# Gate and up of the feed-forward part as seven half-size products per 128 columns, in three of four groups

## The chip, the cores and the metric

One core of one Trainium2 chip. The time is the device time of one launch in microseconds; of the kernel before three runs are known, 3519.23, 3510.82 and 3515.81 us, median 3515.81 us. The profile is of a further execution of 3516.95 us, whose span from the first to the last instruction is 3515.2 us.

## The reference, cut to what matters

One decoder layer runs over 16 meta tokens, 8 short sequences of 4 tokens and a prompt of 2048 tokens: input projection, sliding-window attention and a gated delta rule side by side, their merge, an output projection, and the feed-forward part, which the change is about:

```python
D_MODEL = 1024
D_FF = 2816
hn = _rms_norm(h, norm_ffn)
h = h + (jax.nn.silu(hn @ w_gate) * (hn @ w_up)) @ w_down
```

All of it is float32.

## The kernel before, in words

**Groups.** The prompt is worked through in four groups (`NG`) of 512 tokens. The first group carries the 48 other tokens too (16 meta, 32 of the short sequences), so it is 560 tokens wide, and each of its products is made in two halves of 280 columns (`CA`, `CB`). Activations lie with features on the partitions and tokens along the columns (`MAIN` is the 512 prompt tokens of a group).

**Precision.** TensorE multiplies in a rounded 32-bit format (fp32r). To keep float32 accuracy each operand is split into a rounded part and the rest: ACT makes the rounded part of a weight tile (`weights_hi`, L521, `wh`), DVE the rest (`weights_lo`, L529, `wl`), and each 128x128 weight tile takes three products: rounded x rounded, rounded x rest, rest x rounded (`t_out`, all of them recorded at L768).

**The weight stream.** All weights come in units of 128 partitions x 1024 columns (512 KB, eight 128x128 tiles), 120 per group in the order of `UNITS`, the same for each group: input projection, conv, gates, z, oa/ob, eight `out` units, then for each half `cc` of the feed-forward width (`FFC` = 2 halves of `FFK` = 11 column blocks): `wg` and `wu` of each block, then 11 `down` units. SP loads them (L511) into a ring of two (`raw`), each load waiting until the rest of the unit two before has been made (`lo_done`). Split units lie in a ring of three (`wh`, `wl`); ACT splits unit n+2 once TensorE has begun unit n (`unit_started`, `AHEAD` = 2), and DVE follows it.

**Order on an engine.** Each engine runs its instructions in the order in which they are written; waits on semaphores (`made(...)`) tie them together. Calls `hi_until` (ACT) and `lo_until` (DVE) put the splits of coming units ahead of the step that follows them.

**The feed-forward part.** In the `out` phase DVE adds each of eight output tiles to the residual (`add_columns`, L2114); ACT scales it by the norm's weight and rounds it (L1584, `hnT[0]`), DVE makes the rest (`hn_lo`, L2101, `hnT[1]`), and squares are summed for the norm (L2110). TensorE starts `wg` of block 0 at once, and after it sums the squares over the partitions (L447); DVE (L2141) and POOL (L1679) turn that into one factor per token, which TensorE spreads over the partitions after `wu` of block 0 (L453), and DVE copies it to `hR` (L2145). For each block j: 24 products for gate and 24 for up, each 512 columns wide (in the first group 48 and 48 of 280); DVE multiplies gate by `hR` (L2153, `sg`), ACT applies silu (L1595), DVE multiplies up by `hR` (L2161, `hf`) and then by `sg` (L2165), ACT rounds it (L1598) and DVE makes the rest (L2167) for `down`. Two banks of PSUM each alternate for gate and up, so DVE has a whole block to read them. During the second `down` phase the next group's tokens are loaded and normed.

## Time and profile before

| | |
|---|---|
| median of three runs | 3515.81 us |
| profiled execution / its span | 3516.95 us / 3515.2 us |
| TensorE busy with products | 3422.6 us, 97% of the span, 21860 products |
| DVE, ACT, POOL busy | 1729.8 us (49%), 1256.7 us (36%), 253.2 us (7%) |
| DMA | 298.66 MB, mean 85 GB/s |
| one group's feed-forward part (second group) | from 1505.8 us to about 1874 us |

Products overlap in TensorE, so the duration of one in the profile is longer than the time until the next one starts; where it runs without a pause, the stretch divided by the number of products gives the distance between them. The columns of the windows view are: stretch, length, then for each engine the busy time and in brackets the number of instructions, the granted clock of TensorE as a share of 2.4 GHz, the DMA's busy share and its GB/s.

### The profile page before, as it was taken

To read this page: it belongs to the slowest core of one execution; us is meant where nothing else is said; L and a number is where in the kernel's file an instruction comes from. 1 tells how busy PE (TensorE), PEld (TensorE's weight loads), DVE (VectorE), ACT (ScalarE), POOL (GpSimd) and SP (SyncE) were. 2 spreads that over 40 slices of the span, in tenths; PEclk is the share of its full clock that TensorE was granted. 3 is DMA by queue.
4 is the path that set the end of the run, shared out by engine and by line. 5 is a ranking of instruction groups with operands and counts; after the bars stand their busy time and mean duration, and the time that the engine had idled before them with its cause. 6 is when DMAs were issued, how large, how long until landed. Compare 5 with 4: busy or idle time off the path is not lost.

```text
span 3515.2 us, 52951 instructions
## 1 busy us (share of the span) xinstructions
PE 3422.6 (97%) x21860; PEld 2907.3 (83%) x21860; DVE 1729.8 (49%) x3115; ACT 1256.7 (36%) x2414; POOL 253.2 (7%) x289
## 2 busy tenths in 40 slices
PE   7989999999999999999999999999999999999998
PEld 6877789999998777888878877888878877788886
DVE  4734335543447654544446744554345754454343
ACT  3323334321234544432233544432223544432222
POOL 2211000000003110000002101000000311000000
PEclk9988899999999999999999999999999999999999
DMA  4201013222233111333243211333334211233232
GB/s 172 67 27 56 25 37 99 86 90 85 85 132 112 56 42 50 114 96 96 91 143 110 68 39 47 108 96 96 96 116 139 79 37 43 78 114 96 96 96 81
DMA packets 88574, 298.66 MB, mean 85 GB/s; under 512 B 12288, under 2 KB 14288, under 8 KB 87680
## 3 DMA queue, kind: packets, MB, share of 16 engines
q1 hardware_dynamic: 88336, 295.28, 26.2%
q8 instruction: 175, 2.87, 0.3%
q14 instruction: 63, 0.52, 0.0%
HBM read 283.63 MB, written 12.62 MB: 84 GB/s over the span
## 4 chain that ended last, share of the span: by engine, by line
PE 52%; issue 11%; ACT 2%; DMA 1%; DVE 1%; SPq 0%; POOLq 0%; POOL 0%; DVEq 0%; ACTq 0%
PE bank L768 43%; PE bank L956 1%; PE bank L1193 1%; PE bank L1184 1%; PE bank L1196 1%; PE bank L931 1%; PE bank L1127 1%; PE bank L943 1%; DMA raw<-in_wstream 1%; PE bank L1101 1%; PE bank L1107 0%; PE bank L984 0%; ACT junk L1542 0%; PE bank L1029 0%; PE bank L1138 0%
## 5 line engine op out<-in xcount | busy, mean ns | idle before, releaser
L768 PE MATMUL bank<-hnT,wh 128*128 128x512 f32 (+1 forms) x3520 | 931.4, 352 | 0.0
L529 DVE TENSOR_TENSOR wl<-raw,wh 128x1024 fp32r<-128x1024 f32 x480 | 594.9, 1240 | 653.4 <-ACT wh L521 652.0
L768 PE MATMUL bank<-xnT,wh 128*128 128x512 f32 (+2 forms) x2560 | 742.9, 376 | 10.9 <-DVE d_dT L1955 5.1
L768 PEld LDWEIGHTS bank<-hnT,wh 128*128 128x128 f32 x3520 | 619.4, 188 | 91.4 <-issue 0.2
L521 ACT CAST wh<-raw 128x1024 fp32r<-128x1024 f32 x480 | 500.6, 1043 | 386.5 <-PE bank L768 328.4
L768 PE MATMUL bank<-hnT,wl 128*128 128x512 f32 (+1 forms) x1760 | 622.2, 354 | 0.0
L768 PEld LDWEIGHTS bank<-xnT,wh 128*128 128x128 f32 x2560 | 450.4, 194 | 84.2 <-issue 13.4
L768 PE MATMUL bank<-hid,wh 128*128 128x512 f32 (+1 forms) x1760 | 469.4, 354 | 4.3 <-DVE wl L529 3.1
L768 PE MATMUL bank<-xnT,wl 128*128 128x512 f32 (+2 forms) x1280 | 470.0, 367 | 0.0
L768 PEld LDWEIGHTS bank<-hnT,wl 128*128 128x128 f32 x1760 | 330.6, 188 | 45.8
L768 PEld LDWEIGHTS bank<-hid,wh 128*128 128x128 f32 x1760 | 310.3, 188 | 52.2 <-DVE wl L529 4.7
L768 PE MATMUL bank<-hid,wl 128*128 128x512 f32 (+1 forms) x880 | 311.3, 354 | 0.0
L768 PEld LDWEIGHTS bank<-xnT,wl 128*128 128x128 f32 x1280 | 247.7, 193 | 40.5
L1598 ACT CAST hid<-hf 128x512 fp32r<-128x512 f32 (+1 forms) x88 | 55.5, 630 | 420.2 <-DVE hf L2165 420.2
L768 PEld LDWEIGHTS bank<-hid,wl 128*128 128x128 f32 x880 | 165.9, 189 | 24.1
L768 PE MATMUL bank<-oT,wh 128*128 128x512 f32 (+1 forms) x640 | 169.4, 353 | 4.4 <-DVE oT L2067 3.2
L768 PE MATMUL bank<-mixT,wh 128*128 128x512 f32 (+1 forms) x640 | 169.4, 352 | 1.9 <-DVE mixT L2097 1.9
L1595 ACT ACTIVATE sg<-sg 128x512 f32<-128x512 f32 (+1 forms) x88 | 56.5, 642 | 318.2 <-DVE sg L2153 318.2
L768 PE MATMUL bank<-wh,xnT 128*128 128x512 f32 (+1 forms) x544 | 138.8, 343 | 8.0 <-DMA cm<-in_consts 8.0
L768 PEld LDWEIGHTS bank<-oT,wh 128*128 128x128 f32 x640 | 112.4, 188 | 21.5 <-ACT oT L1558 3.8
L768 PEld LDWEIGHTS bank<-mixT,wh 128*128 128x128 f32 x640 | 112.7, 188 | 18.9 <-ACT mixT L1580 2.1
L1847 DVE SCALAR_TENSOR_TENSOR cy<-pre,pr,cy 128x512 f32<-128x512 f32 x144 | 119.6, 830 | 5.1
(309 smaller groups left out, 3897.5 us busy)
## 6 DMA issues: line engine op xcount, KB each, us to landing
raw<-in_wstream SPq DMA_DIRECT2D x472, 512.0 KB, 3.5
xr<-in_x_prompt SPq DMA_DIRECT2D x16, 512.0 KB, 5.6
hT<-in_xT SPq DMA_DIRECT2D x4, 2048.0 KB, 8.5
out_yp_out<-hT SPq DMA_DIRECT2D x16, 512.0 KB, 2.9
xT<-in_xT SPq DMA_DIRECT2D x3, 2048.0 KB, 12.5
raw<-in_wstream SPq DMA_DIRECT2D x8, 528.0 KB, 3.6
xT<-in_xT SPq DMA_DIRECT2D x2, 1024.0 KB, 9.9
Sb<-in_state_delta SPq DMA_DIRECT2D x1, 2048.0 KB, 9.7
```

The costliest lines, as they stand in the source:

```text
L521: act.copy(wh[n % HL][:, 0:m], raw[:, n % RAW, 0:m]).then_inc(sem("hi_done"), 1)
L529: nc.vector.tensor_tensor(wl[n % HL][:, 0:m], raw[:, n % RAW, 0:m], wh[n % HL][:, 0:m].bitcast(F32), ALU.subtract).then_inc(sem("lo_done"), 1)
L768: ins = nc.tensor.matmul(*a, **k)
L931: last = nc.tensor.matmul(bank[(1, 2)[half]][:, 256 * (y // NKV):256 * (y // NKV + 1)], qTt[ps, x, :], kT[ps, :, :].rearrange("p s n -> p ...
L943: last = nc.tensor.transpose(bank[b][:, P * y:P * (y + 1)], sc[:, x, P * s:P * (s + 1)], c("ident"))
L956: last = nc.tensor.matmul(bank[4][:, HD * y:HD * (y + 1)], pTm[:, 2 * y + s, :], vn[:, s, ps], start=s == 0, stop=s == 1)
L1101: last = nc.tensor.matmul(bank[(5, 7)[y]][dst, w * h:w * (h + 1)], M[src, 2 * h + z, :], Y[src, 2 * h + z, :], start=True, stop=True)
L1127: last = nc.tensor.matmul(bank[(3, 6)[y]][dst, w * h:w * (h + 1)], X[src, 2 * h + z, :], PT[src, 2 * h + z, :], start=True, stop=True)
L1184: last = nc.tensor.matmul(bank[ob][:, P * x:P * (x + 1)], WQ[:, x, P * k:P * (k + 1)], S[:, x, :], start=x == 0, stop=False, skip_group_ch ...
L1595: act.activation(sg[j % 2][:, live], sg[j % 2][:, live], ACT.Silu).then_inc(sem("sg_done"), 1)
L1598: act.copy(hid[0][:, jj, live], hf[j % 2][:, live]).then_inc(sem("hid_hi"), 1)
L1847: ins = v_.scalar_tensor_tensor(out, src(i), w(i), out, ALU.mult, ALU.add)
```

## The change

In groups 2 to 4, blocks 1 to 21 (`PLAIN` = 1 keeps block 0 as it was) no longer make gate and up as two products of full size. Write the block's weights as a 2x2 matrix: row 1 is gate, row 2 is up, and the columns are the two halves of the 1024 features (A11, A12; A21, A22), and the activations as 2x2: feature halves by token halves (256 tokens each). Then seven products of half the features by half the tokens replace eight (a variant of Strassen's algorithm). Each is one `operand_pass`: four 128x128 tiles x three products = 12 products of 256 columns. The four weight sums S1 to S4 and the four sums of activations are new operands.

- The weight sums are made once, in the first group: SP loads the `wg` and `wu` units of each block a second time (`ops_in`), POOL makes the four sums (`ops_out`), and SP writes them to a DRAM tensor `wsum` (1 MB per block). Later groups load S1 to S4 from it and A11, A12, A22 from the weight stream.
- The stream's unit is now 512 columns (`st`) in these blocks; the rings keep their size in bytes: four cells of 512 columns for `raw`, six for `wh` and `wl`. A full unit takes two cells. `AHEAD` is worked out per unit: up to five `st` units ahead.
- The activation sums are made by DVE in the `out` phase (`token_sums`, from `gS`, the scaled residual) and split like the others (`Tm`): ACT four times 1024 columns after the last `hn_lo`, DVE four times.
- PSUM: the passes A11, S2, S3 and A22 add up in one bank (X), S1 and S4 in another (Z), A12 in a third (Y). Values in between are needed as well, so ACT copies the bank (256 columns) after A11, S1, S2 and S3 (`snap`), and TensorE may not add to that bank before. DVE puts the outputs together from these copies and the final banks. Silu, product and split of block j-1 are done between the steps of block j.
- Some semaphores are merged; nothing else of it changes.

```diff
+PLAIN = 1
+OPS = ("A11", "S1", "S2", "S4", "S3", "A12", "A22")
+SUMS = ("S1", "S2", "S3", "S4")
+HC = 512
+def units_of(g):
+    u = ([("a1", i) for i in range(4)] + [("a2", i) for i in range(2)] + [("conv", j) for j in range(NCONV)]
          + [("gate", j) for j in range(16)] + [("z", j) for j in range(4)]
          + [(s, i) for i in range(4) for s in ("oa", "ob")]
          + [("out", i) for i in range(8)])
-for _c in range(FFC):
-    UNITS += [(s, _c * FFK + j) for j in range(FFK) for s in ("wg", "wu")]
-    UNITS += [("down", _c * FFK + i) for i in range(FFK)]
-UNIT_AT = {u: n for n, u in enumerate(UNITS)}
+    for c in range(FFC):
+        for j in range(c * FFK, (c + 1) * FFK):
+            u += [("wg", j), ("wu", j)] if g == 0 or j < PLAIN else [("st", len(OPS) * j + p) for p in range(len(OPS))]
+        u += [("down", c * FFK + i) for i in range(FFK)]
+    return u
...
+RAWC, HLC = 4, 6
...
+def displaced(n, ring):
+    return max(OWNER.get(c - ring, -1) for c in OWNED[n])
+OWNED = [[] for _ in UNITS]
+for _c, _n in OWNER.items():
+    OWNED[_n].append(_c)
+AHEAD = []
+for _n in range(NU):
+    _m = AHEAD[-1] if AHEAD else 0
+    while _m + 1 < NU and displaced(_m + 1, HLC) < _n:
+        _m += 1
+    AHEAD.append(_m)
...
+    def source(n):
+        g, s, i = UNITS[n]
+        if s != "st":
+            return d["wstream"][STREAM[(s, i)]][:, 0:width(n)]
+        j, op = i // len(OPS), OPS[i % len(OPS)]
+        if op in SUMS:
+            return d["wsum"][j][:, HC * SUMS.index(op):HC * (SUMS.index(op) + 1)]
+        u, half = {"A11": ("wg", 0), "A12": ("wg", 1), "A22": ("wu", 1)}[op]
+        return d["wstream"][STREAM[(u, j)]][:, HC * half:HC * (half + 1)]
     def load_until(sp, n):
-        while asked[0] <= min(n, NG * NU - 1):
+        while asked[0] <= min(n, NU - 1):
             k = asked[0]
-            if k >= RAW:
-                sp.wait_ge(sem("lo_done"), k - RAW + 1)
-            m = width(k % NU)
-            sp.dma_start(raw[:, k % RAW, 0:m], d["wstream"][k % NU][:, 0:m]).then_inc(sem(f"raw_in{k % RAW}"), 16)
+            if displaced(k, RAWC) >= 0:
+                sp.wait_ge(sem("lo_done"), displaced(k, RAWC) + 1)
+            sp.dma_start(raw_cell(k), source(k)).then_inc(sem(f"raw_in{CELL[k] % RAWC}"), 16)
...
+        SNAP = {"A11": 1, "S1": 2, "S2": 3, "S3": 4}
+        snap_of = lambda j, op: len(SNAP) * (j - PLAIN) + SNAP[op]
+        RD = {"Z": 1, "Y": 2, "X": 3}
+        rd_of = lambda j, b: len(RD) * (j - PLAIN) + RD[b]
+        BX, BZ, BY = (lambda j: (0, 3)[j % 2]), (lambda j: (1, 4)[j % 2]), (lambda j: (2, 5)[j % 2])
...
+                for j in range(2 * FFK):
+                    weights("wu", min(j + 1, FFK - 1) if j < FFK else j)
+                    if j == 0:
+                        sp.wait_ge(*made("out_ps", 2 * KD))
+                    if j >= 2:
+                        sp.wait_ge(*made("st_sum", j - 1))
+                        sp.wait_ge(*made("st_out", 16 * (j - 2)))
+                        sp.dma_start(d["wsum"][j - 2], ops_out[:, j % 2].rearrange("p s n -> p (s n)")).then_inc(sem("st_out"), 16)
+                    sp.wait_ge(*made("st_in", 32 * j))
+                    for x, name in enumerate(("wg", "wu")):
+                        sp.dma_start(ops_in[:, j % 2, x, :], d["wstream"][STREAM[(name, j)]][:, 0:2 * HC]).then_inc(sem("st_in"), 16)
+                weights("down", FFK)
+                for j in range(2 * FFK - 2, 2 * FFK):
+                    sp.wait_ge(*made("st_sum", j + 1))
+                    sp.wait_ge(*made("st_out", 16 * j))
+                    sp.dma_start(d["wsum"][j], ops_out[:, j % 2].rearrange("p s n -> p (s n)")).then_inc(sem("st_out"), 16)
...
+            def operand_pass(j, op, b, rhs, start=False):
+                w_h, w_l, mm = unit("st", len(OPS) * j + OPS.index(op))
+                out = bank[b][:, 0:HT]
+                for k in range(KD // 2):
+                    ks = slice(P * k, P * (k + 1))
+                    mm(out, w_h[:, ks], rhs(0, k), start=start and k == 0, stop=False, skip_group_check=True)
+                    mm(out, w_h[:, ks], rhs(1, k), start=False, stop=False, skip_group_check=True)
+                    last = mm(out, w_l[:, ks], rhs(0, k), start=False, stop=k == KD // 2 - 1, skip_group_check=True)
+                last.then_inc(sem("st_ps"), 1)
+            def hn_part(k0, cs):
+                return lambda s, k: hnT[s][:, k0 + k, cs]
+            def T_part(j, q):
+                if j == PLAIN:
+                    pe.wait_ge(*made("hn_hi", KD + q + 1))
+                    pe.wait_ge(*made("hn_lo", KD + q + 1))
+                return lambda s, k: Tm[s][:, q, k, :]
+            def seven_products(j):
+                X, Z, Y = BX(j), BZ(j), BY(j)
+                claim(X, "st_rd", rd_of(j, "X"))
+                operand_pass(j, "A11", X, hn_part(0, H1), True)
+                claim(Z, "st_rd", rd_of(j, "Z"))
+                operand_pass(j, "S1", Z, T_part(j, 0), True)
+                pe.wait_ge(*made("snap", snap_of(j, "A11")))
+                operand_pass(j, "S2", X, T_part(j, 1))
+                pe.wait_ge(*made("snap", snap_of(j, "S1")))
+                operand_pass(j, "S4", Z, hn_part(KD // 2, H2))
+                pe.wait_ge(*made("snap", snap_of(j, "S2")))
+                operand_pass(j, "S3", X, T_part(j, 2))
+                claim(Y, "st_rd", rd_of(j, "Y"))
+                operand_pass(j, "A12", Y, hn_part(KD // 2, H1), True)
+                pe.wait_ge(*made("snap", snap_of(j, "S3")))
+                operand_pass(j, "A22", X, T_part(j, 3))
...
+                    act.copy(hnT[0][:, f, live], gS[:, f, :]).then_inc(sem("hn_hi"), 1)
...
+            if not first:
+                act.wait_ge(*made("hn_lo", KD))
+                for q in range(4):
+                    act.copy(Tm[0][:, q], Ts[:, q]).then_inc(sem("hn_hi"), 1)
...
+            def seven_silu(j):
+                act.wait_ge(*made("ga_done", j + 1))
+                act.activation(sg[j % 2][:, live], sg[j % 2][:, live], ACT.Silu).then_inc(sem("sg_done"), 1)
+            def seven_hid(j):
+                act.wait_ge(*made("hf_done", j + 1))
+                act.copy(hid[0][:, j % FFK, live], hf[j % 2][:, live]).then_inc(sem("hid_hi"), 1)
+            def seven_copies(j):
+                behind = j > PLAIN and j % FFK > 0
+                for op in OPS:
+                    hi_until("st", len(OPS) * j + OPS.index(op))
+                    if op not in SNAP:
+                        continue
+                    act.wait_ge(*made("st_ps", product(j, op)))
+                    if op == "A11":
+                        act.wait_ge(*made("hf_done", j - 1))
+                    elif op == "S1" and j > PLAIN:
+                        act.wait_ge(*made("st_rd", rd_of(j - 1, "Y")))
+                    elif op == "S3":
+                        act.wait_ge(*made("hid_lo", j - 1))
+                    dst = {"A11": sg[j % 2][:, H1], "S1": V[:], "S2": sg[j % 2][:, H2], "S3": hf[j % 2][:, H2]}[op]
+                    act.copy(dst, bank[BZ(j) if op == "S1" else BX(j)][:, 0:HT]).then_inc(sem("snap"), 1)
+                    if op == "A11" and behind:
+                        seven_silu(j - 1)
+                    if op == "S2" and behind:
+                        seven_hid(j - 1)
+                if j % FFK == FFK - 1:
+                    seven_silu(j)
+                    seven_hid(j)
...
+            for j in range(2 * FFK if first else 0):
+                pool.wait_ge(*made("st_in", 32 * (j + 1)))
+                if j >= 2:
+                    pool.wait_ge(*made("st_out", 16 * (j - 1)))
+                A = {f"A{1 + x}{1 + y}": ops_in[:, j % 2, x, HC * y:HC * (y + 1)] for x in range(2) for y in range(2)}
+                Q = {n: ops_out[:, j % 2, SUMS.index(n), :] for n in SUMS}
+                tt = nc.gpsimd.tensor_tensor
+                link(tt(Q["S1"], A["A21"], A["A22"], ALU.add))
+                link(tt(Q["S2"], Q["S1"], A["A11"], ALU.subtract))
+                link(tt(Q["S4"], A["A12"], Q["S2"], ALU.subtract))
+                tt(Q["S3"], A["A11"], A["A21"], ALU.subtract).then_inc(sem("st_sum"), 1)
...
+            def scaled_columns(f):
+                dve.wait_ge(*made("out_ps", f + 1))
+                link(v_.tensor_tensor(hT[:, f, MAIN], hT[:, f, MAIN], bank[(0, 3, 1, 4)[f % 4]][:], ALU.add))
+                v_.tensor_scalar(gS[:, f, :], hT[:, f, MAIN], p("nffn", f, 1), None, ALU.mult).then_inc(sem("h_done"), 1)
+            def token_sums(f):
+                T, k, m = (lambda q, k: Ts[:, q, k, :]), f - KD // 2, KD // 2
+                dve.wait_ge(*made("h_done", f + 1))
+                if f == m - 1:
+                    dve.wait_ge(*made("kv_out", 16 * 2))
+                    step(v_.tensor_tensor(Ts[:, 0], gS[:, 0:m, HT:], gS[:, 0:m, 0:HT], ALU.subtract))
+                elif f >= m:
+                    step(v_.tensor_tensor(T(2, k), gS[:, f, HT:], gS[:, k, HT:], ALU.subtract))
+                    settle()
+                    link(v_.tensor_tensor(T(1, k), gS[:, f, HT:], T(0, k), ALU.subtract))
+                    step(v_.tensor_tensor(T(3, k), gS[:, f, 0:HT], T(1, k), ALU.subtract))
...
+            if not first:
+                for q in range(4):
+                    dve.wait_ge(*made("hn_hi", KD + q + 1))
+                    v_.tensor_tensor(Tm[1][:, q], Ts[:, q], Tm[0][:, q].bitcast(F32), ALU.subtract).then_inc(sem("hn_lo"), 1)
...
+            def seven_up(j):
+                dve.wait_ge(*made("st_ps", product(j, "A22")))
+                v_.tensor_tensor(hf[j % 2][:, H1], bank[BX(j)][:, 0:HT], hR[:, H1], ALU.mult).then_inc(sem("st_rd"), 1)
+            def seven_product(j):
+                dve.wait_ge(*made("sg_done", j + 1))
+                dve.wait_ge(*made("st_rd", rd_of(j, "X")))
+                settle()
+                v_.tensor_tensor(hf[j % 2][:, live], hf[j % 2][:, live], sg[j % 2][:, live], ALU.mult).then_inc(sem("hf_done"), 1)
+            def seven_rest(j):
+                dve.wait_ge(*made("hid_hi", j + 1))
+                v_.tensor_tensor(hid[1][:, j % FFK, live], hf[j % 2][:, live], hid[0][:, j % FFK, live].bitcast(F32), ALU.subtract).then_inc(sem("hid_lo"), 1)
+            def seven_sums(j):
+                behind = j > PLAIN and j % FFK > 0
+                R, gj, uj = hR, sg[j % 2], hf[j % 2]
+                for op in OPS:
+                    lo_until("st", len(OPS) * j + OPS.index(op))
+                    if op == "A11" and behind:
+                        seven_up(j - 1)
+                    elif op == "S2" and behind:
+                        seven_product(j - 1)
+                    elif op == "S3":
+                        dve.wait_ge(*made("st_ps", product(j, "S4")))
+                        dve.wait_ge(*made("snap", snap_of(j, "S2")))
+                        v_.tensor_tensor(gj[:, H2], gj[:, H2], bank[BZ(j)][:, 0:HT], ALU.add).then_inc(sem("st_rd"), 1)
+                        if behind:
+                            seven_rest(j - 1)
+                    elif op == "A12":
+                        dve.wait_ge(*made("snap", snap_of(j, "S3")))
+                        link(v_.tensor_tensor(uj[:, H2], uj[:, H2], V[:], ALU.add))
+                        step(v_.tensor_tensor(uj[:, H2], uj[:, H2], R[:, H2], ALU.mult))
+                    elif op == "A22":
+                        dve.wait_ge(*made("st_ps", product(j, "A12")))
+                        v_.tensor_tensor(gj[:, H1], gj[:, H1], bank[BY(j)][:, 0:HT], ALU.add).then_inc(sem("st_rd"), 1)
+                        dve.wait_ge(*made("st_rd", rd_of(j, "Y")))
+                        v_.tensor_tensor(gj[:, live], gj[:, live], R[:, live], ALU.mult).then_inc(sem("ga_done"), 1)
+                if j % FFK == FFK - 1:
+                    seven_up(j)
+                    seven_product(j)
+                    seven_rest(j)
```

## Rows read from the trace of the kernel before

**Rows 1.** The page: busy time of each engine over the span.

```profile
PE 3422.6 (97%) x21860; PEld 2907.3 (83%) x21860; DVE 1729.8 (49%) x3115; ACT 1256.7 (36%) x2414; POOL 253.2 (7%) x289
```

**Rows 2.** Chain of waits, 1500 to 1640 us: start, length, what.

```profile
1518.86 121.17 PE bank L768 x524
```

**Rows 3.** Windows over gate-and-up stretches, products that read hnT alone; first group, then second.

```profile
666.30:790.10 123.80, 123.79 (x960) 1.00 0.29 89
1518.60:1629.60 111.00, 110.99 (x480) 1.00 0.32 96
1691.00:1813.00 122.00, 122.00 (x528) 1.00 0.28 87
```

**Rows 4.** Windows, all engines: PE, PEld, DVE, ACT, POOL, clock, DMA share, GB/s.

```profile
666.30:790.10 123.80, 123.80 (x963) 123.80 (x962) 58.04 (x85) 33.84 (x42) 0.00 (x0) 1.00 0.29 89
1518.60:1629.60 111.00, 111.00 (x483) 90.23 (x482) 54.55 (x63) 32.99 (x42) 0.00 (x0) 1.00 0.32 96
```

**Rows 5.** Groups by form of the narrow products, whose mean is not their distance.

```profile
L768 PE MATMUL bank<-wh,xnT 128*128 128x264 f32 x272 | 50.5, 284 | 0.0
L768 PE MATMUL bank<-xnT,wh 128*128 128x48 f32 x256 | 44.5, 272 | 5.1 <-DVE d_dT L1955 5.1
```

**Rows 6.** Windows, PE alone: 96 products of 264 columns; 24 of 48 columns.

```profile
1900.80:1912.50 11.70, 11.70 (x97) 1.00 0.53 175
482.20:484.80 2.60, 2.60 (x25) 1.00 0.05 9
```

**Rows 7.** Groups by form: ACT and DVE with 256 columns out of PSUM.

```profile
L1360 ACT COPY qkv<-bank 128x256 f32<-128x256 f32 x16 | 6.0, 374 | 13.4 <-PE bank L768 13.4
L1759 DVE TENSOR_TENSOR qkv<-bank,st 128x256 f32<-128x256 f32 x32 | 13.6, 423 | 90.6 <-PE bank L956 90.6
```

**Rows 8.** Timeline, second group, block 0: start, duration, engine, line, idle before.

```profile
1520.40 0.63 ACT L1595 ACTIVATE sg<-sg 128x512 f32<-128x512 f32 x1 [10.19 <-DVE sg L2153]
1520.94 1.04 ACT L521 CAST wh<-raw 128x1024 fp32r<-128x1024 f32 x1
1522.01 1.23 DVE L529 TENSOR_TENSOR wl<-raw,wh 128x1024 fp32r<-128x1024 f32 x1 [1.64 <-ACT wh L521]
1523.15 0.68 DVE L2161 TENSOR_TENSOR hf<-bank,hR 128x512 f32<-128x512 f32 x1
1523.97 0.69 DVE L2165 TENSOR_TENSOR hf<-hf,sg 128x512 f32<-128x512 f32 x1
```

**Rows 9.** Timeline, second group, from the last out tile to block 1.

```profile
1506.01 0.69 DVE L2114 TENSOR_TENSOR hT<-hT,bank 128x512 f32<-128x512 f32 x1 [1.39 <-PE bank L768]
1512.34 0.16 DVE L2141 TENSOR_SCALAR hr<-bank 128x4 f32<-128x4 f32 x1 [1.98 <-PE bank L447]
1512.64 1.01 POOL L1679 TENSOR_TENSOR hr<-hr,nhalf 128x4 f32<-128x4 f32 x1 [121.50 <-DVE hr L2141]
1517.80 1.06 PE L453 MATMUL bank<-cm,hr 128*128 128x128 f32 x8
1518.90 0.69 DVE L2145 COPY hR<-bank 128x512 f32<-128x512 f32 x1 [6.39 <-PE bank L453]
```

**Rows 10.** Timeline: a pause of TensorE in the third group.

```profile
2001.42 0.66 PE L984 MATMUL bank<-cm,post 128*128 128x128 f32 x4 [2.17 <-ACT post L1458]
```

**Rows 11.** Windows, PE alone: behind that pause, behind one of 2.11 us, behind a like one.

```profile
2002.70:2006.00 3.30, 3.30 (x29) 0.50 0.02 5
2637.60:2640.90 3.30, 3.30 (x9) 0.50 0.93 384
1191.10:1194.50 3.40, 3.35 (x46) 1.00 0.00 0
```

**Rows 12.** Timeline, second group: POOL and DVE both at work in SBUF.

```profile
1115.22 1.21 POOL L1637 TENSOR_TENSOR rt<-qkv,rope_t 128x320 f32<-128x320 f32 x1
1115.61 1.90 DVE L529 TENSOR_TENSOR wl<-raw,wh 128x1024 fp32r<-128x1024 f32 x1
```

**Rows 13.** DMA issues: count, KB each, median us to landing.

```profile
raw<-in_wstream SPq DMA_DIRECT2D x472, 512.0 KB, 3.5
```

More of the change, by code:

```diff
@@ L305, in program @@
     cst = place("cst", [P, NCONV, NB * (CW - 1)])
-    raw = place("raw", [P, RAW, UW])
-    wh = [place(f"wh{s}", [P, UW], F32R) for s in range(HL)]
-    wl = [place(f"wl{s}", [P, UW], F32R) for s in range(HL)]
+    raw = place("raw", [P, RAWC // 2, UW])
+    wh = [place(f"wh{s}", [P, UW], F32R) for s in range(HLC // 2)]
+    wl = [place(f"wl{s}", [P, UW], F32R) for s in range(HLC // 2)]
     r_xn = region(2 * KD * W * 4)
@@ L312, in program @@
     mixT = [place(f"mixT{s}", [P, KD, W], F32R, r_xn + s * KD * W * 4) for s in range(2)]
+    HT = GROWS // 2
+    Tm = [place(f"Tm{s}", [P, 4, KD // 2, HT], F32R, r_xn + s * 4 * KD // 2 * HT * 4) for s in range(2)]
+    V = place("V", [P, HT], F32, r_xn + 2 * 4 * KD // 2 * HT * 4)
+    assert (2 * 4 * KD // 2 + 1) * HT <= 2 * KD * W
+    ops_in = place("ops_in", [P, 2, 2, 2 * HC], F32, r_xn)
+    ops_out = place("ops_out", [P, 2, len(SUMS), HC], F32, r_xn + 2 * 2 * 2 * HC * 4)
+    assert (2 * 2 * 2 + 2 * len(SUMS)) * HC <= 2 * KD * W
     r_gt = region(16 * W * 4)
@@ L516, in weights_hi @@
         assert n == rounded[0]
[L517 to L521 removed]
+        act.wait_ge(sem(f"raw_in{CELL[n] % RAWC}"), 16 * ARRIVED[n])
+        if displaced(n, HLC) >= 0:
+            act.wait_ge(sem("unit_started"), displaced(n, HLC) + 2)
+        act.copy(hi_cell(n), raw_cell(n)).then_inc(sem("hi_done"), 1)
         rounded[0] += 1
@@ L684, in group @@
         last_group = g == NG - 1
+        H1, H2 = slice(NS, NS + HT), slice(NS + HT, W)
+        seven = lambda j: not first and j >= PLAIN
+        product = lambda j, op: len(OPS) * (j - PLAIN) + OPS.index(op) + 1
+        SNAP = {"A11": 1, "S1": 2, "S2": 3, "S3": 4}
[3 more added lines that the diff above has]
+        BX, BZ, BY = (lambda j: (0, 3)[j % 2]), (lambda j: (1, 4)[j % 2]), (lambda j: (2, 5)[j % 2])
         quarters_of = lambda t: QUARTERS_S if t == "S" else QUARTERS_0 if first else QUARTERS
@@ L1381, in gate_logits @@
                 if first:
-                    act.copy(gate[:, j, SM], bank[4][:, B4S:B4S + NS]).then_inc(sem("gate_eS"), 1)
+                    act.copy(gate[:, j, SM], bank[4][:, B4S:B4S + NS]).then_inc(sem("gate_e"), 1)
                 act.copy(gate[:, j, MAIN], bank[0][:]).then_inc(sem("gate_e"), 1)
@@ L1583, in scalar @@
                 act.wait_ge(*made("h_done", (1 + F) * (f + 1)))
-                act.activation(hnT[0][:, f, live], hT[:, f, live], ACT.Copy, scale=p("nffn", f, 1)).then_inc(sem("hn_hi"), 1)
+                if first:
+                    act.activation(hnT[0][:, f, live], hT[:, f, live], ACT.Copy, scale=p("nffn", f, 1)).then_inc(sem("hn_hi"), 1)
+                else:
+                    act.copy(hnT[0][:, f, live], gS[:, f, :]).then_inc(sem("hn_hi"), 1)
                 if f >= 3:
@@ L1592, in scalar @@
                     j = cc * FFK + jj
+                    if seven(j):
+                        seven_copies(j)
+                        continue
                     hi_until("wg", j)
@@ L1609, in scalar @@
                     act.activation((acc if f == 0 else sq[f % 2])[:, live], hT[:, f, live], ACT.Square).then_inc(sem("ysq_done"), 1)
+                    if f == 4 and first:
+                        act.wait_ge(*made("st_out", 16 * 2 * FFK))
                     if f >= 4 and not last_group:
@@ L1701, in lo_until @@
             def lo_until(name, i):
-                while split[0] <= min(g * NU + UNIT_AT[(name, i)] + AHEAD, NG * NU - 1):
+                while split[0] <= AHEAD[NUM[(g, name, i)]]:
                     weights_lo(dve, split[0])
@@ L2135, in vector @@
                     j = cc * FFK + jj
+                    if seven(j):
+                        seven_sums(j)
+                        continue
                     lo_until("wg", j)
```

176 lines of the change are left out of this document (106 added, 70 removed).

## The prediction

> **What bounds the kernel now.** I read the page's busy times first. TensorE is at its products for 97% of the span, DVE for 49%, ACT 36%, POOL 7% [rows 1]. A busy share alone doesn't make a bound, so next the chain of waits in the second group's feed-forward part: from 1518.86 us it is one piece of 121 us of products on TensorE, with no other engine in it [rows 2]. Then the windows over the gate-and-up stretches: busy in all of 111.0 us, granted clock 1.00 [rows 4]. So what counts there is how many products there are and how far apart they start. Divide length by count: 110.99/480 = 231.2 ns and 122.00/528 = 231.1 ns for 512 columns, 123.79/960 = 128.9 ns for the first group's 280 [rows 3]. The other engines have room: in 10 blocks DVE is busy 54.6 of 111 us, ACT 33.0 [rows 4].
>
> **The main term.** A block had 48 products of 512 columns and gets 7 x 12 = 84 of 256. 21 blocks in each of three groups change: 3024 products go, 5292 come. The old ones cost 3024 x 231.1 ns = 698.8 us. No row has 256 columns back to back. The line through 280 and 512 has a slope of (231.1 - 128.9)/232 = 0.4405 ns a column, which gives 128.9 - 24 x 0.4405 = 118.3 ns. The 264-column products start 11.70/96 = 121.9 ns apart [rows 5, 6] and give 121.9 - 8 x 0.4405 = 118.4 ns, the value I take. Bounds: 108 ns, what even 48 columns cost (2.60/24) [rows 5, 6], so a floor under narrow products, and 121.9 ns above. New cost 5292 x 118.4 = 626.6 us, gain **72.2 us** (53.7 at 121.9 ns, 127 at 108). The column work alone falls by an eighth; the gain is less than that, 10%, since each product pays a fixed part (118.4 for 256 against 231.1/2 = 115.6).
>
> The Trainium skill, "TensorE: Matmul & The Clock Gate", section "Back-to-back issue gap", gives N/2.4 + 2.5 ns, so 109.2 ns for 256 columns, and its "LDWEIGHTS" section P/1.2, so 106.7 ns, as the floor. By it the new products would cost 577.9 us, near rival 4. The trace is slower than that formula at both widths it has: 231 against 215.8 ns, and 128.9 against 119.2.
>
> **Does TensorE keep its pace inside a block?** A pass takes 12 x 118.4 ns = 1.42 us, a block 9.95 us. Three times per block a bank may only be added to when ACT has copied it, one pass (1.42 us) after it was filled, and once for bank Z. Durations: an ACT instruction of 512 columns takes 0.63 us but the next starts 0.54 us after it, DVE's 1024 columns 1.23 us with 1.14 between starts [rows 8]: successors overlap by 0.09 us. 256 columns take ACT 0.37 and DVE 0.42 us [rows 7], 0.28 and 0.33 us apart. A DVE instruction that needs the one before it starts 0.14 us after its end (1523.15 + 0.68 to 1523.97) [rows 8]. Per block DVE makes seven splits of 512 columns (0.60 each), three other full-width operations (0.60) and five half-width ones (0.33), with two such pauses: 4.2 + 1.8 + 1.65 + 0.3 = 8.0 us, 80% of a block. ACT: 9 x 0.54 + 4 x 0.28 = 6.0 us. Both fit, but they are in order, so I lay them end to end over a steady block, with A11's start as 0. DVE's last three steps (S3, A12, A22 of the block before) hold 5.1 us of work in 4.3 us, so the gate of block j-1 is complete at 2.0. ACT has copied A11 by then (1.6 to 2.0; needed at 2.84), does silu (to 2.6), the split for step S1 (to 3.2) and the copy of S1 (to 3.5; needed at 4.27). Copy S2: 4.4 to 4.8 (needed 5.69), copy S3: 7.3 to 7.7 (needed 8.54). Each has 0.8 us to spare. The weight splits are up to five passes ahead (7.1 us) and late by 2.9 at most. A load of 512 KB lands after 3.5 us [rows 13]; the new ones are of half that size, and their cells come free 6 us before ACT wants them. Cost: 0, at most the 0.8 us and again as much per block if these spares are gone (rivals).
>
> **The start of each later group's feed-forward part.** Here ACT and DVE get new work that nothing covers. Take the start of `wg` 0 (1505.8 us in the second group) as 0. The new operations in the `out` phase (scaling, three sums of 256 columns per tile) take DVE about 2.1 us per tile; it is idle for 1.39 us ahead of each add [rows 9] and again while ACT splits. Laid end to end behind the last tile, hnT is complete at 4.85, just when TensorE wants it (21 x 0.231). Then ACT rounds the four activation sums (4 x 1024 columns, 0.95 apart: 4.9 to 8.7) and DVE makes their rest (to 10.6), before either turns to weights: ACT splits A11 and S1 (8.7 to 9.8), DVE follows (to 11.7), and only then DVE computes the norm's factor, which it did at 1512.34, that is 6.5 [rows 9]. POOL takes 1.01 us for it [rows 9]: ready at 13.1. TensorE wanted it at 12.0 (1517.80). **1.1 us late.** A11 of block 1 starts at 13.9. Next hR is copied (14.2 to 14.9), gate 0 scaled (15.7), silu 0 (16.3), ACT splits S2 and S4 (17.4), DVE follows (18.1), up 0 and the product (19.6), ACT rounds it (20.3), splits S3 and A12 (21.3) and only then copies A11: 21.6. TensorE would have begun S2 at 16.75, and here a copy can't be late without a cost. **4.9 us.** Behind it ACT is level again. Together 6.0 us x 3 = 18 us. Bounds: 3 if only the first wait stands, 30 if ACT needs a second block to catch up.
>
> Such a pause may drop the clock. After two pauses of some 2.1 us the granted clock was 0.50 (1.2 GHz) for 3.3 us (after one at 2001.42 [rows 10]), after a third it stayed at 1.00 (2.4 GHz) [rows 11]. I count one such stretch per group: half of 3.4 us lost, 1.7 x 3 = 5 us; bounds 0 and 10.
>
> **First group.** POOL makes four sums of 512 columns per block. Its 320 columns took 1.21 us beside DVE [rows 12], so 1.9 us each and 7.7 us per block, in blocks of 96 x 128.9 ns = 12.4 us: it fits, and nothing waits for it but the two last writes. Traffic: two more units read and 1 MB written make 3.1 MB per block, 254 GB/s; 384 GB/s flowed in one window [rows 11]. SP has these DMAs ahead of weight loads, but it is two units (12.4 us) ahead. DVE waits where both want SBUF: 1.90 instead of 1.23 us [rows 12], 0.67 more in four operations per block; with its 58.0 us per 10 blocks [rows 4] that is 8.5 of 12.4 us. Cost: 0. Bounds: 0 and 22.
>
> The Trainium skill, "SBUF — State Buffer", section "SBUF: two separate sides", says that the pair of ports that DVE and GpSimd share is locked for a whole instruction, for DVE also where both inputs are in SBUF; it speaks against moving sums to POOL. The stretched DVE row agrees with it.
>
> **Sum.** 3516.95 (the profiled execution) - 72.2 + 18 + 5 = 3467.8 us. The median of the runs is 1.1 us lower than that execution: **3467 us**, 1.4% less.
>
> **Rivals.**
> 1. *The copies are late by part of a pass in every block.* The estimate above rests on instructions overlapping by 0.09 us. Without that DVE has 9.3 us per block and the spare 0.8 us is used up. Half a microsecond late in 60 blocks: 3467 + 30 = 3497 us. For it: the last three steps already hold more than they can. Against: 2 us of idle DVE in each block. 0.15.
> 2. *The same place, but slower than before.* ACT's copy of S1 comes a whole pass late in each block, since silu, on which it is queued, waits for DVE's gate: 60 x 1.42 = 85 us, so 3552 us. It ends above 3516 once the lateness passes 49/60 = 0.8 us, which needs the gate 1.6 us later than I have it. For and against as in 1; late raw tiles, for which ACT waits in front of a copy, would add to it. 0.11.
> 3. *The shared port slows the first group.* If DVE waits for a whole POOL operation (1.9 us) at each of four operations, a block has 5.8 + 7.6 = 13.4 us of DVE against 12.4: 22 us, 3489 us. Against: the row shows 0.67 us. 0.07.
> 4. *Narrow products come at the 108 ns of the 48-column row.* Gain 127 us, 3412 us. Against it is the line through three widths. 0.03.
> 5. *No difference.* Lateness and start-up eat just the gain. 0.04.
>
> The forecast has 0.60, and its own range is 3450 to 3485 (products at 117.5 to 120 ns, start-up 10 to 27 us). About 0.2% (7 us) is what can be told from no change here. Faster: 0.60 + 0.15 + 0.07 + 0.03 = 0.85, less 0.02 of rival 1's tail: 0.83. Same: 0.05. Slower: 0.12. The range for 8 in 10 runs from 3447 up to 3510, which takes in rivals 1 and 3.
>
> **What would show it.** In the gate-and-up windows of groups 2 to 4: 84 products per block, 9.95 us a block, TensorE without idle time. In a timeline from the last `out` tile: a wait of about 1 us before the spread of the norm's factor and of about 5 us at S2 of block 1, ended by ACT's copy. First group: its stretches still 123.8 and 136 us. It is wrong if passes start over 1.5 us apart in a steady block, and then the releaser tells which: ACT's copy (rivals 1 and 2) or DVE's `wl` (the splits, which I hold to be early).

## The result

3477.79 us is the median of the changed kernel (3474.17 to 3478.18, 4 runs) against 3517.35 us of the kernel before on the same chip (3510.82 to 3519.23, 4 runs): ratio 0.9889, interval 0.9871 to 0.9906, so 1.1% less and clear of no change. The forecast was 3467 us, 1.4% less. The profiled execution has a span of 3475.5 us against 3515.2, so 39.7 us less, at a mean granted clock of 0.979 against 0.981.

The profile after, its page: busy time of the engines, the products of gate and up that read hnT and Tm, and the new loads. It answers to [rows 1] and [rows 13].

```profile
PE 3360.6 (97%) x24128; PEld 2973.7 (86%) x24128; DVE 1974.8 (57%) x3757; ACT 1477.1 (42%) x2993; POOL 388.9 (11%) x377
...
L876 PE MATMUL bank<-Tm,wh 128*128 128x256 f32 x2016 | 372.0, 284 | 13.8 <-DVE wl L609 13.8
...
raw<-wsum SPq DMA_DIRECT2D x252, 256.0 KB, 3.4
raw<-in_wstream SPq DMA_DIRECT2D x189, 256.0 KB, 2.7
```

TensorE stays the bound with 2268 products more (24128 - 21860) and 62 us less busy. DVE went from 49 to 57%, ACT from 36 to 42%. The row of the products that read the activation sums (`Tm`) also holds an idle time: 13.8 us, which is three pauses of 4.6 us.

Windows over the second group's two gate-and-up stretches, all engines for the second and TensorE alone for the first and for two pieces of it (columns as in [rows 4] and [rows 6]):

```profile
1691.44:1801.12 109.68, 109.68 (x924) 109.67 (x923) 86.42 (x158) 70.06 (x139) 0.00 (x0) 1.00 0.59 176
```

```profile
1520.88:1627.72 106.84, 102.26 (x843) 0.97 0.58 173
...
1528.57:1533.50 4.93, 4.93 (x23) 0.50 0.68 205
```

The second stretch is what was forecast for all: 11 blocks of 84 products whose 923 distances fill 109.68 us, so 118.83 ns a product and 9.98 us a block, with no idle time of TensorE. It took 122.00 us before [rows 3]. The first stretch has ten such blocks and should take 839 x 118.83 ns = 99.7 us; it takes 106.84. Its loss sits at block 1, the first one made in seven products. TensorE's timeline there, then ACT's:

```profile
1519.96 1.16 PE L517 MATMUL bank<-cm,hr 128*128 128x128 f32 x8 [0.54 <-POOL hr L1869]
...
1523.71 0.28 PE L876 MATMUL bank<-Tm,wl 128*128 128x256 f32 x1
1528.57 0.80 PE L876 MATMUL bank<-Tm,wh 128*128 128x256 f32 x2 [4.58 <-DVE wl L609]
```

```profile
1523.20 1.12 ACT L602 CAST wh<-raw 128x512 fp32r<-128x512 f32 x2
1526.59 0.62 ACT L1786 CAST hid<-hf 128x512 fp32r<-128x512 f32 x1 [2.27 <-DVE hf L2442]
1527.11 1.13 ACT L602 CAST wh<-raw 128x512 fp32r<-128x512 f32 x2
1528.15 0.36 ACT L1765 COPY sg<-bank 128x256 f32<-128x256 f32 x1
```

The row names DVE's `wl`, which came last by the profile, but the `wl` of this step was there by 1525.13, 3.4 us before; the product that follows starts 0.06 us after the end of ACT's copy of A11 (L1765, 1528.15 + 0.36), which had stood behind block 0's rounding (L1786) and two splits. So it is the queue of ACT that the forecast named. Behind it the clock is 0.50 (1.2 GHz): 23 instructions in 4.93 us, 0.214 us each. The same stretch takes 106.94 and 107.30 us in the third and fourth group: the pause is as long there, 4.58 and 4.60 us, but 5.1 and 6.0 us at half clock lie behind it.

Another pause comes at the end of the same stretch, ahead of the first `down` product. The chain of waits has it in the third group (first fence, columns as in [rows 2]), the timelines of TensorE and then of DVE in the second:

```profile
2327.13 99.52 PE bank L876 x816
2426.65 2.04 issue
2428.70 171.61 PE bank L876 x1189
```

```profile
1627.72 0.28 PE L876 MATMUL bank<-Tm,wl 128*128 128x256 f32 x1
1630.04 0.70 PE L876 MATMUL bank<-hid,wh 128*128 128x512 f32 x2 [2.05 <-issue]
```

```profile
1628.91 0.69 DVE L2400 TENSOR_TENSOR sg<-sg,hR 128x512 f32<-128x512 f32 x1
1629.52 0.42 DVE L2364 TENSOR_TENSOR hf<-bank,hR 128x256 f32<-128x256 f32 x1
1630.30 0.69 DVE L2370 TENSOR_TENSOR hf<-hf,sg 128x512 f32<-128x512 f32 x1 [0.36 <-ACT sg L1744]
```

"issue" says only that the profile shows no releaser. What ends just before is L2364, DVE's last read of bank X of the pass's last block (0.10 us before TensorE starts). That bank is bank 0 in the first pass (block 10, an even number) and bank 3 in the second; `down` claims bank 0 first. The pause is there in the first pass of each later group (2.05, 2.04 and 2.07 us) and in no second pass.

The first group, whose windows answer to [rows 4]:

```profile
666.30:790.10 123.80, 123.80 (x961) 123.59 (x961) 66.69 (x85) 33.94 (x42) 64.19 (x42) 1.00 0.70 247
860.20:996.10 135.90, 135.90 (x1057) 135.90 (x1056) 68.28 (x85) 34.90 (x43) 61.21 (x40) 1.00 0.69 250
```

TensorE has no idle time in it; DVE went from 58.0 to 66.7 us and POOL from nothing to 64.2, both under the products.

**The account.** Gain of the products: 698.8 - 5292 x 0.11883 = 70.0 us. Per later group come off, in distances of starts: 0.8 us ahead of block 1, where the norm's factor is spread (13.85 us from the last `out` product to block 1's first, against 13.04); 7.1 us in the stretch (106.84 - 99.7; 7.2 and 7.6 in the next two groups), of which 4.7 are the pause and 2.4 lie behind it (23 x (0.214 - 0.119) = 2.2 of them are the clock; 2.5 and 2.9 in the next two); 2.2 us ahead of `down` (2.32 instead of a usual 0.11). Over three groups that is 2.4 + 22.0 + 6.6 = 31.0, which leaves 39.0. The two spans counted from the first product of block 1 in the first group differ by 41.5 (2848.9 against 2807.4); of the 2.5 more, 1.2 are the end behind the last `down` product (15.6 us against 16.8), the rest smaller differences up and down. That first product came 1.8 us later in this execution (668.12 against 666.31), and this gives the 39.7. It isn't the change's doing: in two experiments with the same first group it came at 666.28 and 664.67.

### The profile page after: what moved, and what is told of

Its sections match the earlier page's. It is cut to its first block and busy times, and to the rows that moved or that the text cites. A ratio compares the mean times of both kernels' runs of the same rounds, so it can differ in the third digit from the quotient of the medians.

```text
span 3475.5 us, 60004 instructions
## 1 busy us (share of the span) xinstructions
PE 3360.6 (97%) x24128; PEld 2973.7 (86%) x24128; DVE 1974.8 (57%) x3757; ACT 1477.1 (42%) x2993; POOL 388.9 (11%) x377
## 5 line engine op out<-in xcount | busy, mean ns | idle before, releaser
L609 DVE TENSOR_TENSOR wl<-raw,wh 128x512 fp32r<-128x512 f32 (+1 forms) x795 | 750.4, 951 | 644.2 <-ACT wh L602 641.7
L602 ACT CAST wh<-raw 128x512 fp32r<-128x512 f32 (+1 forms) x795 | 636.0, 808 | 483.4 <-PE bank L876 417.5
L876 PE MATMUL bank<-hnT,wh 128*128 128x256 f32 (+2 forms) x3016 | 583.5, 291 | 0.0
L876 PEld LDWEIGHTS bank<-hnT,wh 128*128 128x128 f32 x3016 | 476.3, 189 | 4.3 <-issue 0.2
L876 PE MATMUL bank<-hnT,wl 128*128 128x256 f32 (+2 forms) x1508 | 438.6, 291 | 0.0
L876 PE MATMUL bank<-Tm,wh 128*128 128x256 f32 x2016 | 372.0, 284 | 13.8 <-DVE wl L609 13.8
L876 PEld LDWEIGHTS bank<-Tm,wh 128*128 128x128 f32 x2016 | 313.3, 191 | 14.4 <-ACT sg L1765 14.4
L876 PEld LDWEIGHTS bank<-hnT,wl 128*128 128x128 f32 x1508 | 285.2, 189 | 2.1
L876 PE MATMUL bank<-Tm,wl 128*128 128x256 f32 x1008 | 285.8, 284 | 0.0
L876 PEld LDWEIGHTS bank<-Tm,wl 128*128 128x128 f32 x1008 | 192.2, 191 | 0.0
```

The costliest lines, as they stand in the source:

```text
L602: act.copy(hi_cell(n), raw_cell(n)).then_inc(sem("hi_done"), 1)
L609: nc.vector.tensor_tensor(lo_cell(n), raw_cell(n), hi_cell(n).bitcast(F32), ALU.subtract).then_inc(sem("lo_done"), 1)
L876: ins = nc.tensor.matmul(*a, **k)
```

## The experiments

Time is given as median, ratio to the kernel before on the same chip with its interval, and span. To take out the chance in the beginning, I compare spans counted from the first product of block 1 in the first group ("length"): 2848.9 us before, 2807.4 after. A length is that of one execution. The kernel before took 3514.58 us on the chip of experiments 1, 2, 3 and 5, and 3515.35 us on that of 4, 6, 7 and 8.

**1. The last block's bank X is bank 6, which `down` claims last.**

```diff
-        BX, BZ, BY = (lambda j: (0, 3)[j % 2]), (lambda j: (1, 4)[j % 2]), (lambda j: (2, 5)[j % 2])
+        BX, BZ, BY = (lambda j: 6 if j == FFK - 1 else (0, 3)[j % 2]), (lambda j: (1, 4)[j % 2]), (lambda j: (2, 5)[j % 2])
```

> Bank X of block 10 is bank 6 instead of bank 0. Theory A: the pause of about 2.05 us ahead of the first down unit in each later group comes from its claim on bank 0, which DVE's last read of block 10 (L2364) still holds. Then the three pauses go, and the time falls by 3 x 2.05 = 6 us against the changed kernel (profiled execution about 3470 span). Rival: down waits there for hid (split of the last blocks) or for its weight tiles: then the pauses stay and the time is the same. The cc = 1 start of down, where X is bank 3, has no such pause and doesn't change in either case.

3467.57 us, 0.9866 (0.985 to 0.9883), span 3464.9; length 2798.6, 8.8 less than after. TensorE's timeline at the place of the pause:

```profile
1625.96 0.28 PE L876 MATMUL bank<-Tm,wl 128*128 128x256 f32 x1
1626.07 0.62 PE L876 MATMUL bank<-hid,wh 128*128 128x512 f32 x2
```

The three pauses are gone, so the claim of bank 0 made them: 3 x 2.2 = 6.6 us. The other 2.1 us are a pause ahead of a `down` product at 1814.66 that the changed kernel's trace has and this one hasn't. The kernel before has a like one in the third group [rows 11], and experiment 6, without any seven-product block, has one of 2.07 us there, so it isn't the change's. The pauses at S2 (4.6 us, the third product of block 1) and the clock behind them stay.

**2. Two plain blocks at the start of each later group instead of one.**

```diff
-PLAIN = 1
+PLAIN = 2
...
```

> Block 1 is left plain too (PLAIN = 2). Theory B: the 4.6 us pause at S2 of the first seven-product block is ACT's queue at the start of the part, which is level again a block later. Then it shrinks to about 1 us (block 1's product is rounded 2.4 us after its last product, then two splits, then the copy at 3.8 where 2.84 is wanted), the clock stays at 1.00, and per group 3.6 + 2.5 us come back for 11.1 - 9.98 = 1.1 us given up: 5 us per group, 15 us in all, span about 3460. Rival: every first seven-product block has this pause whatever stands ahead of it, since its first copy always waits for the block before to be finished: then the pause stays at 4.6 us and the time rises by 3.4 us.

3468.10 us, 0.9866 (0.9851 to 0.9881), span 3466.7; length 2798.2, 9.2 less. The pause at S2 and its half clock are gone (22 us in three groups), three blocks fewer have seven products (3 x 1.1 us given back), and new losses take about half of it, so that less came than the 15 us expected: 1.4 to 2.0 us per group in the first stretch, where the first seven-product blocks wait for ACT's copies (0.98 us of it at 1536.55), and the pause ahead of `down`, now 2.6 us, with half a clock behind it in two groups of three. Windows of TensorE over the 3.4 us after that pause, groups 2 to 4:

```profile
1626.52:1629.92 3.40, 3.40 (x9) 0.56 0.33 130
2421.61:2425.01 3.40, 3.40 (x9) 0.53 0.35 122
3217.49:3220.89 3.40, 3.40 (x15) 1.00 0.34 134
```

9 instructions instead of 15 in the first two: 6 x 0.23 = 1.4 us each time.

**3. ACT's and DVE's order around block 0.** The splits for S2 and S4 go ahead of gate and silu of block 0, the copy of A11 of block 1 ahead of the rounding of block 0's product, and that rounding and its rest between the steps of block 1.

```diff
@@ ACT
-                    hi_until("st", len(OPS) * j + OPS.index(op))
+                    if not (j == PLAIN and op == "A11"):
+                        hi_until("st", len(OPS) * j + OPS.index(op))
...
+                    if j == PLAIN and op == "A11":
+                        hi_until("st", len(OPS) * j)
-                    if op == "S2" and behind:
+                    if op == "S2" and j % FFK > 0:
...
+                    if not first:
+                        hi_until("wu", j)
@@ DVE
-                        if behind:
+                        if j % FFK > 0:
...
```

> Only the order on ACT and DVE around block 0 is changed in groups 2 to 4: splits of S2 and S4 ahead of silu 0, the copy of A11 of block 1 ahead of the rounding of block 0's product, that rounding and its rest later, between the steps of block 1. Theory B: the pause at S2 of block 1 falls from 4.6 us to at most 0.5, and with it goes the half clock behind it (2.5 us per group): 3 x 6.6 = 20 us less, span about 3456. The wait of 1 us ahead of the spread stays. Rival: the clock's drop is not a matter of this pause: then only 3 x 4.1 = 12 us go, and the windows behind block 1's start still show 0.5.

3466.80 us, 0.9862 (0.9848 to 0.9877), span 3465.0; length 2797.3, 10.1 less. The window over the first stretch, and TensorE's timeline at its start and ahead of `down`:

```profile
1521.75:1622.11 100.36, 100.30 (x842) 1.00 0.59 180
1622.20:1685.00 62.80, 60.75 (x256) 0.97 0.33 96
```

```profile
1518.70 0.40 PE L876 MATMUL bank<-hnT,wl 128*128 128x512 f32 x1
1520.84 1.16 PE L517 MATMUL bank<-cm,hr 128*128 128x128 f32 x8 [1.74 <-POOL hr L1876]
```

The stretch is 100.4 us instead of 106.8: the 4.58 us and the half clock came from the order of ACT's and DVE's instructions around block 0, 6.5 us here and 5.9 and 6.5 in the next groups, 19 us together, where 20 were expected. Some 8 of them are given back: the norm's factor is later still, since more splits stand ahead of it on DVE (1.74 us of waiting, 15.05 us from the last `out` product), and the 2.05 us ahead of `down` now have half a clock behind them in each group, where they had none in the changed kernel (`down` takes 62.7 us instead of 61.2): 3.6 and 4.6 us in three groups.

**4. The norm's factor right after DVE's first rest of the sums.** The wait and the `tensor_scalar` move from behind the weight splits into the loop over `Tm`, at q = 0.

```diff
+                    if q == 0:
+                        dve.wait_ge(*made("hsum_ps", 1))
+                        v_.tensor_scalar(hr[:, F:NT + F], bank[3][:, F:NT + F], 1.0 / DM, EPS, ALU.mult, ALU.add).then_inc(sem("hpre_done"), 1)
...
```

> Only the norm factor (L2418) is moved ahead of three of the four rests of the activation sums on DVE, in groups 2 to 4. The spread then starts when wu of block 0 ends, 0.8 us earlier per group (13.85 back to 13.04 us from the last out product to the spread's end). If nothing hangs on it, 2.4 us less than the changed kernel. Rival, which I hold likelier: block 1 starts 0.8 us earlier, but its copy of A11 still waits for block 0's product on ACT and DVE; that chain starts with the spread too, so it moves along by 0.8 us and the gain stands; only if the chain starts with DVE's splits (done at 1518.6) is the pause at S2 longer by 0.8 us and the gain zero.

3475.77 us, 0.9886 (0.987 to 0.9903), span 3473.4. This one was run after experiment 5. 13.04 us from the last `out` product to block 1's first, as before the change, so the 0.8 us were that factor's place. The pause at S2 is still 4.65 to 4.67 us; the times can't tell 2 us, the trace can.

**5. Experiments 1, 3 and 4 together.**

> All three together: bank 6 for X of block 10, the order of e4, and DVE's norm factor (L2418) ahead of three of the four rests of the activation sums. If the parts don't touch each other: 6 + 20 + 3 x 0.8 = 28 us less than the changed kernel, span about 3447, 2.0% under the kernel before. If the norm factor's delay only moves the wait to the next one, 26 us. Rival: the pauses hide others behind them (raw tiles, DVE), then less than 20 us.

**3447.99 us** (3445.1 to 3452.0), 0.981 (0.9795 to 0.9825), span 3445.0; length 2778.1, 29.3 less than after and 70.8 less than before. Windows of the second group's first stretch and of the `down` behind it:

```profile
1519.63:1620.39 100.76, 100.56 (x843) 100.03 (x842) 81.20 (x147) 63.98 (x128) 0.00 (x0) 1.00 0.61 185
1620.50:1682.00 61.50, 61.50 (x268) 49.80 (x267) 21.60 (x27) 12.88 (x15) 0.00 (x0) 1.00 0.35 106
```

The clock is 1.00 in both. The single gains (8.8 with 2.1 of chance in it, 10.1 and about 2) sum to less than the 29.3, since in 3 the other two pauses grew into what it had freed. Of the products' 70.0 us nearly all is there, but the 70.8 flatter it: the first stretches of the three groups (100.8, 100.6 and 100.5 us where 99.7 would do) still lose 2.8 us together, and the profiled execution of the kernel before had three stretches at half clock between 1500 and 3460 us (at 2002.65, 2637.53 and 2815.02) that this one hasn't. By medians on the same chip the gain is 66.6 us. This is the fastest kernel of the study.

**6. All of the preparation, no seven-product block.** Weight sums in the first group and activation sums in the later ones are made, and every block is computed in its two plain units.

```diff
-PLAIN = 1
+PLAIN = 22
...
```

> PLAIN = 22: no block is made with seven products, but the weight sums in the first group, the scaled residual, the activation sums and their splits are all still made. It prices the preparation alone. Theory: it is hidden but for the late norm factor, 0.8 us per group, so 2.4 us more than the kernel before (span about 3518, ratio 1.001). Rival 3 of the prediction (POOL's sums hold up DVE in the first group) would add up to 22 us there: first group's gate-and-up stretches longer than 123.8 and 136.1 us.

3517.48 us (10 runs), 1.0006 (0.9997 to 1.0015), span 3515.4. Of the preparation, 0.7 us per later group show (13.77 us where 13.04 were), which is 2.2 us or 0.06%, inside the interval. The sums cost nothing that the times can tell, in either place.

**7 and 8. One, and three, further ACT copies of 512 columns ahead of the copy of S1** in the 57 seven-product blocks that follow another one in the same half. They write scratch tiles that nothing reads. The diff is that of one; for three it has `range(3)`.

```diff
+                    if op == "S1" and behind:
+                        act.wait_ge(sem("act_step"), act_steps[0])
+                        for r in range(1):
+                            act_steps[0] += 1
+                            act.copy((sq[0], sq[1], acc)[r][:, live], cm[:, 0:GROWS]).then_inc(sem("act_step"), 1)
...
```

> One more ACT copy of 512 columns (constants to a tile that is free then) right ahead of the copy of S1 in every seven-product block but the first of each half, 57 blocks in all. If a copy has the 0.8 us to spare that the prediction worked out, 0.54 us more cost nothing: the same time as the changed kernel, blocks still 9.98 us. If the spare is under 0.3 us (rival 1's place), each block gets at least 0.25 us longer, 14 us or more in all.

3498.21 us (3491.81 to 3499.24), 0.9948 (0.9933 to 0.9962), span 3489.7. By the copy alone, one would be free: in the changed kernel copies start 0.04 us after the end of their pass and end 0.86 us (median) before TensorE needs them. But from about the fourth seven-product block of a stretch on, a block takes 10.3 us instead of 9.98 (924 products in 112.6 us), and in 51 of the 57 blocks ACT's copy of S1 ends only 0.05 us before TensorE starts S4: TensorE is waiting for it. The copy comes 1.0 us later in the block, not 0.54, because silu ahead of it starts 2.50 us into the block instead of 1.89 (medians), and what silu waits for is DVE's gate.

Why the gate is late shows when one follows ACT and DVE from one copy of S1 to the next. This is a block of experiment 7: ACT, then DVE, then TensorE at the start of S4.

```profile
1765.99 0.36 ACT L1770 COPY V<-bank 128x256 f32<-128x256 f32 x1
1766.54 0.62 ACT L602 CAST wh<-raw 128x512 fp32r<-128x512 f32 x1 [0.19 <-DMA raw<-in_wstream]
...
1768.52 0.62 ACT L1748 CAST hid<-hf 128x512 fp32r<-128x512 f32 x1 [1.09 <-DVE hf L2376]
1769.05 1.14 ACT L602 CAST wh<-raw 128x512 fp32r<-128x512 f32 x2
...
1775.01 0.63 ACT L1744 ACTIVATE sg<-sg 128x512 f32<-128x512 f32 x1 [0.81 <-DVE sg L2406]
1775.55 0.60 ACT L602 CAST wh<-raw 128x512 fp32r<-128x512 f32 x1
1776.06 0.61 ACT L1769 COPY sq<-cm 128x512 f32<-128x512 f32 x1
1776.58 0.36 ACT L1770 COPY V<-bank 128x256 f32<-128x256 f32 x1
```

```profile
1767.19 0.69 DVE L609 TENSOR_TENSOR wl<-raw,wh 128x512 fp32r<-128x512 f32 x1 [0.91 <-ACT wh L602]
1767.80 0.69 DVE L2376 TENSOR_TENSOR hf<-hf,sg 128x512 f32<-128x512 f32 x1
1769.70 1.29 DVE L609 TENSOR_TENSOR wl<-raw,wh 128x512 fp32r<-128x512 f32 x2 [1.21 <-ACT wh L602]
...
1773.84 0.41 DVE L2404 TENSOR_TENSOR sg<-sg,bank 128x256 f32<-128x256 f32 x1
```

```profile
1766.07 0.28 PE L876 MATMUL bank<-Tm,wl 128*128 128x256 f32 x1
1766.41 0.51 PE L876 MATMUL bank<-hnT,wh 128*128 128x256 f32 x2
```

Copy of S1, ACT's split, DVE's rest of it, DVE's product of block j-1, its rounding on ACT, ACT's next split, then ten operations of DVE one behind the other (5.28 us from the first's start to the gate's end), silu, split, spare copy, copy of S1: each starts 0.03 us after the end of the one it needs or overlaps with its predecessor. Only the split at 1766.54 waits a little more, for a load, and this block is 0.3 us longer than the next ones. Without that wait the loop takes 10.30 us, and nothing in it waits for TensorE. The spare copy has 0.52 us of it (1776.06 to 1776.58). So I estimate the same loop in the changed kernel at 9.78 us, 0.20 less than TensorE's 9.98: that is the room for work at this place, not 0.86. By it three copies give 9.78 + 1.56 = 11.34 us a block, which the next run measures.

ACT's waits for loads grew too. Its wait list in this kernel, then in the changed one (waiting instruction, what for, us in total, times, longest):

```profile
ACT wh L602 <- DMA raw<-in_wstream: 106.7, 67, 11.0
```

```profile
ACT wh L602 <- DMA raw<-in_wstream: 61.8, 21, 8.4
```

But of the 69 us of such waits inside the seven-product stretches 64 lie just ahead of the copy of A11, outside the loop: DVE's ten operations run through beside them. Loads lengthen single blocks, as the one above, and aren't the common 0.3 us.

> Three such copies, 1.62 us. With 0.86 us to spare (copy of S1 ends at 1621.26 us in the changed kernel, S4 is due at about 1622.1) the pass S4 begins 0.76 us late in each of 57 blocks: 43 us more than the changed kernel, blocks about 10.7 us, and TensorE's pause ahead of S4 is ended by ACT's copy. If lateness is carried from block to block (silu and splits queue behind it) it is more, up to 1.6 us per block, 92 us. If ACT had a whole pass to spare there: under 15 us.

3556.72 us, 1.0118 (1.0102 to 1.0133), span 3553.3: 11.33 us a block, as the loop has it, 1.36 more than in the changed kernel and 0.6 more than the 0.76 that the copy's own spare would have let one expect. TensorE's timeline in a block and its wait list:

```profile
1763.08 0.28 PE L876 MATMUL bank<-Tm,wl 128*128 128x256 f32 x1
1764.46 0.51 PE L876 MATMUL bank<-hnT,wh 128*128 128x256 f32 x2 [1.10 <-ACT V L1770]
```

```profile
PE bank L876 <- ACT V L1770: 59.3, 57, 1.2
```

This is what rival 2 describes: a copy late by over 0.8 us per block, and the kernel is slower than before the change.

## Why the prediction was right, and where it was off

**The bound and the main term.** Right. Only TensorE's products count, and 256 columns come 118.83 ns apart where the line through three widths gave 118.4: 70.0 us instead of 72.2, or 2.2 us of the 10.8 us between forecast and median. Rival 4 (108 ns) is out. The Trainium skill, "TensorE: Matmul & The Clock Gate", section "Back-to-back issue gap", gives N/2.4 + 2.5 ns, which it calls the gap of a single isolated product, and so 109.2 ns; the trace of products in a row doesn't agree, 118.83 ns at this width, nor at the two of before.

**TensorE keeps its pace in a steady block.** Right: no idle time in 11 blocks, 0.86 us left to each copy where 0.8 was worked out. The overlap of 0.09 us between successors, on which rival 1 hung, held (silu, 0.63 us long, at 1775.01 and the split behind it at 1775.55). But the sum laid DVE's and ACT's steps end to end in one block and never closed them into a loop over two, and as a statement on the room of a block its 0.8 us is too wide. The loop takes some 9.78 us of 9.98: 0.2 us more of work in it and TensorE no longer sets the pace, as experiments 7 and 8 show. Rival 1 was nearer than its spare of 0.8 us made it look.

**The start of a later group.** Right in both places and near in size: 0.8 us for the factor (1.1), 4.7 us for the copy of A11 (4.9), 5.5 together against 6.0. Experiments 4 and 3 took away one each, the first by moving what the step had named, the second by reordering ACT and DVE around it.

**The clock.** Right that it falls, too small: the stretch of 3.3 us had been read behind pauses of 2.1 us [rows 11], and with 4.6 us the granted clock was low for 6.8 us, 1.9, 1.7 and 0.8 of them still in the pause. What lay behind it cost 2.4, 2.5 and 2.9 us instead of 1.7.

**The missed term: 6.6 us.** The step that failed is the one that closes the sum of waits at block 1: "Together 6.0 us x 3 = 18 us". ACT is indeed level again a block later, but the wait ahead of `down`, 2.2 us per group, stands in no term. I followed the banks inside gate and up and never asked who claims bank X after its last block. Before, too, the last block's banks were given to `down`, but at its end only an `up` product stood open; now gate's two late sums and the gate itself are ahead of the read of X on DVE. Experiment 1 shows it.

**The first group.** Right: 0. Rival 3 is out by the windows, and experiment 6 measures it together with the activation sums: 1.0006 (0.9997 to 1.0015). A POOL sum of 512 columns took 1.29 us mostly and 2.15 beside a DVE split; DVE's time in the window rose by 8.7 us, to 54% of it, and nothing waited for that.

Account from the sum for the profiled execution (3467.8 us) to the one measured (3477.66), in us: products +2.2, start -1.5, clock +2.8, `down` +6.6, block 1 of the first group reached later by chance +1.8, small differences elsewhere -2.5, time outside the span +0.4. That is 9.8 of 9.9. No large errors cancel in it: the missed term is two thirds of the difference, the rest are sizes.

## What to carry to other kernels

When a stretch on the bound engine gets shorter, follow every shared buffer over the stretch's last block into the next phase: what was last read there decides the start of the next phase, and a bank that this phase claims last costs nothing. Put an instruction that another engine waits for ahead of those that only prepare later work, and remove pauses together, since a single one taken away lets others grow and each may drop the clock. A spare read at one instruction isn't the room of its engine: follow the waits of two engines from that instruction to the same one a block later, add up the loop and compare it with the block. Here 0.86 us were left at the copy and 0.20 us in the loop.

## What the runs showed of the hardware

The same pause doesn't always cost the same. In the changed kernel and in experiment 4 the 2.05 us ahead of `down` had no half clock behind them in any group; in experiment 7 they had a stretch of 3.4 us in one group of three, in experiments 3 and 8 in all three. 2.6 us had one in two of three groups of experiment 2 (0.56, 0.53, 1.00). The pause of 4.6 us came with 6.8 us at half clock in 13 of 15 cases (the changed kernel and experiments 1, 4, 7 and 8) and with 3.4 us in the other two. So a pause of 2 us was worth 2 to 3.5 us in these runs, and one of 4.6 us, 6.5 to 7.6 in the changed kernel and experiment 4.
